# Splitting the products of the second attention into halves, and four small moves around the scan layer and the final norm

## The reference, cut to what matters

```python
def second_block(x, ...):
    # i = 0: scan layer, then keys and values for all later layers
    x = mamba2_layer(x, a_norm_g, a_w_in, conv_w, conv_b, ..., gate_norm_g, w_out)
    k, v = shared_kv_2(x, kv_norm_g, w_kv)
    # i = 1: second attention
    x = diff_attention_layer(x, k, v, norm_g, w_in, lam_qk, sub_g, w_out, lambda_init)
    return rms_norm_2(x, final_norm_g)

def diff_attention_layer(x, k, v, norm_g, w_in, lam_qk, sub_g, w_out, lambda_init):
    qg = rms_norm_2(x, norm_g) @ w_in          # 1024 columns of queries, 1024 of gates
    ...
    scores = einsum("bhiqd,bhikd->bhiqk", qb, k) * scale - slopes * dist     # i = 0, 1
    probs = softmax(where(allowed, scores, -inf))
    weights = probs[:, :, 0] - lam * probs[:, :, 1]
    out = einsum("bhqk,bhke->bqhe", weights, v)
    out = rms_norm_2(out, sub_g) * (1.0 - lambda_init)
    return x + (out * silu(gate)) @ w_out

def mamba2_layer(...):
    zxbcdt = rms_norm_2(x, norm_g) @ w_in      # z, x, B, C and 32 columns of dt
    ...                                        # convolution, chunked scan in 8 groups
    y = gated_group_rms_norm(y, z, gate_norm_g)  # a norm in each of the 8 groups
    return x + y @ w_out
```

## Time and profile before

| | us |
|---|---|
| median of three runs | 2121.86 |
| the profiled execution | 2124.95 |
| its span in the trace | 2123.1 |
| PE busy | 2009.2 (95%) |
| DVE busy | 1387.2 (65%) |
| ACT busy | 856.8 (40%) |
| POOL busy | 267.7 (13%) |
| mean granted clock of PE | 0.972 |

### The profile page before, as it was taken

The page is one execution under the profiler, slowest core; times in us unless marked ns, Lnnn a source line. Parts: engine busy times, 40 slices in busy tenths (PEclk is TensorE's granted clock), DMA queues, the critical chain, the costliest instruction groups (busy, mean ns, idle before and its releaser), DMA issues.

```text
span 2123.1 us, 24820 instructions
## 1 busy us (share of the span) xinstructions
PE 2009.2 (95%) x9332; PEld 1577.4 (74%) x9332; DVE 1387.2 (65%) x2060; ACT 856.8 (40%) x1332; POOL 267.7 (13%) x241
## 2 busy tenths in 40 slices
PE   6789999999999999999999999899999999999987
PEld 4667878888888776777888887677777777876555
DVE  7895457636644448747635654888888887346865
ACT  4454333222233347733222233444444444235653
POOL 4130000000000000010000001234333332000002
PEclk9986999999999999999999999999999999999998
DMA  5354323232233220022233223121222213321002
GB/s 197 107 134 111 122 72 101 85 113 91 86 92 111 88 90 10 1 90 89 85 104 101 96 82 109 53 65 56 80 73 77 80 56 104 101 79 50 21 26 75
DMA packets 79479, 178.33 MB, mean 84 GB/s; under 512 B 17664, under 2 KB 31104, under 8 KB 79360
## 3 DMA queue, kind: packets, MB, share of 16 engines
q1 hardware_dynamic: 75648, 169.46, 26.0%
q0 software_dynamic: 3424, 6.23, 1.1%
q10 hardware_dynamic: 288, 1.05, 0.2%
HBM read 169.43 MB, written 7.27 MB: 83 GB/s over the span
## 4 chain that ended last, share of the span: by engine, by line
PE 74%; DVE 14%; ACT 6%; issue 4%; DMA 1%; POOL 0%; SPq 0%; POOLq 0%; DVEq 0%; ACTq 0%
PE psum L410 19%; PE psum L413 19%; PE psum L411 18%; DVE wl L381 2%; PE psum L430 2%; PE psum L431 2%; PE psum L433 2%; PE psum L780 1%; PE psum L782 1%; PE psum L781 1%; ACT wh L370 1%; PE psum L1617 1%; PE psum L978 1%; DVE S L2451 1%; DVE Bs L2009 1%
## 5 line engine op out<-in xcount | busy, mean ns | idle before, releaser
L381 DVE TENSOR_TENSOR wl<-raw,wh 128x1024 fp32r<-128x1024 f32 (+3 forms) x337 | 387.6, 1151 | 385.6 <-ACT wh L370 385.1
L410 PE MATMUL psum<-xh,wh 128*128 128x512 f32 x1480 | 590.3, 399 | 3.6 <-DVE ust L592 1.8
L413 PE MATMUL psum<-xh,wl 128*128 128x512 f32 x1480 | 579.7, 392 | 1.9 <-DVE wl L381 1.9
L411 PE MATMUL psum<-xl,wh 128*128 128x512 f32 x1480 | 578.7, 391 | 0.0
L370 ACT ACTIVATE wh<-raw 128x1024 fp32r<-128x1024 f32 (+3 forms) x337 | 315.4, 937 | 290.3 <-PE psum L413 181.3
L410 PEld LDWEIGHTS psum<-xh,wh 128*128 128x128 f32 x1480 | 279.7, 189 | 78.3 <-issue 13.6
L413 PEld LDWEIGHTS psum<-xh,wl 128*128 128x128 f32 x1480 | 279.2, 189 | 63.6 <-DVE wl L381 4.5
L411 PEld LDWEIGHTS psum<-xl,wh 128*128 128x128 f32 x1480 | 279.5, 189 | 59.7 <-issue 2.9
L529 POOL TENSOR_TENSOR rs<-rs,sq 128x512 f32<-128x512 f32 x49 | 67.2, 1371 | 1123.7 <-ACT sq L514 1123.0
L410 PE MATMUL psum<-fh,wh 128*128 128x512 f32 x352 | 139.1, 395 | 0.0
L413 PE MATMUL psum<-fh,wl 128*128 128x512 f32 x352 | 139.1, 395 | 0.0
(11 more groups left out here) (449 smaller groups left out, 3099.5 us busy)
## 6 DMA issues: line engine op xcount, KB each, us to landing
raw<-d_w SPq DMA_DIRECT2D x224, 512.0 KB, 3.5
raw<-d_w SPq DMA_DIRECT2D x32, 384.0 KB, 3.0
raw<-d_w SPq DMA_DIRECT2D x48, 256.0 KB, 2.6
raw<-d_w SPq DMA_DIRECT2D x32, 320.0 KB, 2.9
Mt<-d_kd SPq DMA_DIRECT2D x64, 64.0 KB, 2.4
bc<-d_bc SPq DMA_DIRECT2D x8, 256.0 KB, 3.6
d_ud<-ust SPq DMA_DIRECT2D x8, 256.0 KB, 2.6
U<-d_ud POOLq DMA_DIRECT2D x64, 32.0 KB, 2.4
```

The lines of the kernel that those rows point to most:

```text
L381: dve.e.tensor_tensor(K.wl[n % NH][:, 0:COLS[n]], K.raw[n % RAW][:, 0:COLS[n]], K.wh[n % NH][:, 0:COLS[n]].bitcast(F32), ALU.subtract).the ...
L410: pe.e.matmul(b[:, :], WH[:, o:o + P], XH, start=(k == k0), stop=False)
L411: pe.e.matmul(b[:, :], WH[:, o:o + P], XL, start=False, stop=False)
L413: mm = pe.e.matmul(b[:, :], WL[:, o:o + P], XH, start=False, stop=(k == k1 - 1))
```

## The change

In `att2_order` each of the 14 products becomes two steps in neighbouring iterations: the first four slices (12 matmuls) in the old iteration, the other four one iteration later, after that iteration's scores. The new `product_half` issues them into the same bank, and other matmuls go to other banks between them. What reads the result moves one iteration later (`queryB`, `gateB`, `gateT`, `gateC`). The splits get steps of their own: the high part (`H`) at the end of the iteration before the first half, the low part (`L`) behind `combine` in the iteration of the first half. `sumsq` is listed at the head of the iteration after, which is the same place in PE's own order.

In the scan layer, `norm` of group 7 comes before `out` 2 of that group, and the low parts of group 6 are made by DVE and no more by POOL. At the layer's start, ACT loads the table of Ln and Exp ahead of its splits, and DVE takes the variance ahead of its splits.

In the final norm, POOL adds six squares and not seven, and PE sums the seventh with a matmul of its own into the same bank.

```diff
@@ mamba_order
-            ("update", 7, 0), ("update", 7, 1), ("squares", 7, 0), ("scale", 6, 0), ("out", 7, 2), ("sums", 7, 0),
-            ("out", 7, 3), ("norm", 7, 0), ("root", 7, 0), ("newton", 7, 0), ("scale", 7, 0), ("out", 7, 4)]
+            ("update", 7, 0), ("update", 7, 1), ("squares", 7, 0), ("scale", 6, 0), ("norm", 7, 0), ("out", 7, 2),
+            ("sums", 7, 0), ("out", 7, 3), ("root", 7, 0), ("newton", 7, 0), ("scale", 7, 0), ("out", 7, 4)]
@@ att2_order
-    at = {(k * 31 + 6) // 13: x for k, x in enumerate(dense)}
+    first = {(k * 31 + 6) // 13: x for k, x in enumerate(dense)}
+    second = {n + 1: x for n, x in first.items()}
     out = [("query", 0), ("queryB", 0), ("query", 1), ("queryB", 1)]
+    out.append((first[0][0] + "H", first[0][1]))
...
-        if n in at:
-            what, m = at[n]
-            out.append((what, m))
+        if n in first:
+            out.append(first[n])
+        if n in second:
+            what, m = second[n]
+            out.append((what + "2", m))
             later.setdefault((n + 1, "first"), []).append((what + "B", m))
...
             out.append(("combine", n - 2))
+        if n in first:
+            out.append((first[n][0] + "L", first[n][1]))
         if 0 <= n - 3 < 32:
             out.append(("keep", n - 3))
+        if n + 1 in first:
+            out.append((first[n + 1][0] + "H", first[n + 1][1]))
+        if 0 <= n - 3 < 32:
             if (n - 3) % 4 == 3:
                 hd = (n - 3) // 4
-                for k, what in enumerate(("mix", "sumsq", "rs", "tailA", "tailB", "split")):
-                    later.setdefault((n + 1 + k, "last"), []).append((what, hd))
+                for k, what in ((1, "mix"), (3, "rs"), (4, "tailA"), (5, "tailB"), (6, "split")):
+                    later.setdefault((n + k, "last"), []).append((what, hd))
                 later.setdefault((n + 2, "first"), []).append(("square", hd))
+                later.setdefault((n + 3, "first"), []).append(("sumsq", hd))
@@ new
+def product_half(K, pe, name, m, bank, x, freed, half):
+    if half == 0:
+        take(pe, bank, freed)
+        pe.begun = next_unit(K, pe, name, "T", m, 0)
+    n, WH, WL = pe.begun
+    b = K.bank[bank]
+    pe.wait_ge("hi", n + 1)
+    for k in range(4 * half, 4 * half + 4):
+        o = k * P
+        XH, XL = x(k)
+        pe.e.matmul(b[:, :], WH[:, o:o + P], XH, start=(k == 0), stop=False)
+        pe.e.matmul(b[:, :], WH[:, o:o + P], XL, start=False, stop=False)
+        pe.wait_ge("lo", n + 1)
+        mm = pe.e.matmul(b[:, :], WL[:, o:o + P], XH, start=False, stop=(k == 7))
+    if half:
+        mm.then_inc(K.S["unit"], 1)
@@ add_squares, sum_squares
-    for k in range(1, 8):
+    for k in range(1, 7 if b == 6 else 8):
...
-    pe.wait_ge("acc", 7 * (b + 1))
+    pe.wait_ge("acc", 7 * b + 6 if b == 6 else 7 * (b + 1))
...
-    pe.e.matmul(K.bank[bank][:, :], K.con("ones"), K.acc[:, :], start=True, stop=True).then_inc(K.S["ssum"], 1)
+    mm = pe.e.matmul(K.bank[bank][:, :], K.con("ones"), K.acc[:, :], start=True, stop=(b != 6))
+    if b == 6:
+        pe.wait_ge("sq", 8 * b + 8)
+        mm = pe.e.matmul(K.bank[bank][:, :], K.con("ones"), K.sq[1][:, :], start=False, stop=True)
+    mm.then_inc(K.S["ssum"], 1)
@@ mamba_first_act, mamba_first_dve
+    act.log_exp()
     split_hi(K, act, UNIT[("a_w_in_2", "N32", 6144, 0)] + 1 + LA)
...
+    variance(K, dve, 4, 5, 1e-5)
     split_lo(K, dve, UNIT[("a_w_in_2", "N32", 6144, 0)] + 1 + LA)
-    rsqrt(K, dve, 4, 5, 1e-5)
+    dve.wait_ge("ny", 5)
+    newton(K, dve, K.ny[:, :], K.nv[:, :], K.ns[:, :], K.rs[:, :]).then_inc(K.S["rs"], 1)
@@ scan_scale_dve, mamba_pool
-        if g == 7:
+        if g >= 6:
...
-        elif what == "scale" and g < 7:
+        elif what == "scale" and g < 6:
```

More of the change, by code:

```diff
@@ L184, in att2_order @@
     dense = [x for m in range(8) for x in ([("query", m + 2)] if m < 6 else []) + [("gate", m)]]
-    at = {(k * 31 + 6) // 13: x for k, x in enumerate(dense)}
-    assert len(at) == 14 and max(at) < 33
+    first = {(k * 31 + 6) // 13: x for k, x in enumerate(dense)}
+    second = {n + 1: x for n, x in first.items()}
+    assert len(first) == 14 and max(second) < 33 and not set(first) & set(second)
     out = [("query", 0), ("queryB", 0), ("query", 1), ("queryB", 1)]
+    out.append((first[0][0] + "H", first[0][1]))
     later = {}
@@ L571, in newton, with variance @@
     return dve.e.scalar_tensor_tensor(out=out, in0=s, scalar=1.5, in1=y, op0=ALU.add, op1=ALU.mult)
+def variance(K, dve, b, bank, eps):
+    dve.wait_ge("ssum", b + 1)
+    dve.e.tensor_scalar(K.nv[:, :], K.bank[bank][:, :], 1.0 / D, eps, ALU.mult, ALU.add).then_inc(K.S["nv"], 1)
 def rsqrt(K, dve, b, bank, eps, by_token=None):
@@ L578, in rsqrt @@
         dve.e.tensor_scalar(K.tv[:, :], K.bank[by_token][:, 0:4], 1.0 / D, eps, ALU.mult, ALU.add).then_inc(K.S["tv"], 1)
-    dve.wait_ge("ssum", b + 1)
-    dve.e.tensor_scalar(K.nv[:, :], K.bank[bank][:, :], 1.0 / D, eps, ALU.mult, ALU.add).then_inc(K.S["nv"], 1)
+    variance(K, dve, b, bank, eps)
     if b in BY_TOKEN:
@@ L2592, in att2_pe @@
     for what, m in ATT2_ORDER:
-        if what == "query" and m > 1:
-            product(K, pe, "b_w_in_2", m, B2[(what, m)], x, ("aqc", m + 1))
-        elif what == "gate":
-            product(K, pe, "b_w_in_2", 8 + m, B2[(what, m)], x, ("agg", m + 1))
+        if what in ("query", "query2") and m > 1:
+            product_half(K, pe, "b_w_in_2", m, B2[("query", m)], x, ("aqc", m + 1), int(what == "query2"))
+        elif what in ("gate", "gate2"):
+            product_half(K, pe, "b_w_in_2", 8 + m, B2[("gate", m)], x, ("agg", m + 1), int(what == "gate2"))
         elif what == "out":
@@ L2622, in att2_act @@
     for what, m in ATT2_ORDER:
-        if what in ("query", "gate", "out"):
-            split_hi(K, act, done(*tile2(what, m)) + LA)
+        if what in ("queryH", "gateH", "out") or (what == "query" and m < 2):
+            split_hi(K, act, done(*tile2(what.strip("H"), m)) + LA)
         elif what == "gateT":
@@ L2663, in att2_dve @@
     for what, m in ATT2_ORDER:
-        if what in ("query", "gate", "out"):
-            split_lo(K, dve, done(*tile2(what, m)) + LA)
+        if what in ("queryL", "gateL", "out") or (what == "query" and m < 2):
+            split_lo(K, dve, done(*tile2(what.strip("L"), m)) + LA)
         elif what == "queryB":
```

## The result

The changed kernel takes 2091.61 us, the median of four runs (2090.12 to 2093.63), against 2122.31 us for the kernel before in the same session (2120.57 to 2123.85): a ratio of 0.9856, interval 0.9839 to 0.9873. It is faster by 30.7 us. The forecast was 15.5 us and its range ended at 2096, 4.4 us above what came. The profiled execution took 2093.63 us with a span of 2091.8, so the traces differ by 31.3 us of span.

What follows compares the result with a forecast made beforehand. PE, busy 95% of the span, was taken to bound the kernel. Savings of 12.3 (loop), 0.4 (scan start), 1.5 (scan end) and 1.3 us (final norm) summed to 15.5, giving a median of 2106.4 us; range 2096 to 2115.

Steps and rivals of the forecast that it cites:

- Loop, halves: Second attention's loop: 28 half products give PE work in 27 iterations instead of 14, cutting idle time; about 8 us saved.
- Loop, the splits' places: Second attention's loop: moving high and low parts removes VectorE's 32.0 us stand; counted as nothing beyond PE's other gains.
- Loop, idle of what remains: Second attention's loop: five iterations left without a half product keep 1.4 us of PE idle each, 7 us.
- Loop, clock: Second attention's loop: 21.6 us at 1.2 GHz lose 10.8; about half spared, 5 us, bounds 0 and 9.
- Loop, openings and table loads: Second attention's loop: 14 more product openings cost 1.7 us; four more ScalarE table loads, 5.1 us, hidden in spare time.
- Behind the loop: After the second attention's loop: gate 7's second half lies ahead of head 6's sum of squares; 1 us saved.
- Scan layer, start: Scan layer's start: earlier table load and variance let Newton begin sooner; 0.4 us saved taken, possibly 0.6 us lost.
- Scan layer, end: Scan layer's end: group 7's earlier variance shortens the 2.77 us wait before the last pair; 1.5 us saved, bounds 0 and 2.8.
- Final norm: Final norm: GpSimd's last addition goes, so PE starts sooner after ScalarE's last square; 1.3 us saved, bound 0.7.
- More: Rival, chance 0.07: clock stays up in the loop and at both scan layer ends, loop idle down to 4: 2095 us.
- The three on the other side: Rivals of smaller or no gain: VectorE sets pace, 2114 (0.16); loop gives nothing, 2118.7 (0.08); ScalarE sets pace, 2132 (0.04).
- Waits only move: Rival, chance 0.16: VectorE becomes the loop's pace, so the loop gives only 2 to 7 us: 2114 us.

Runs made afterwards that it cites:

- Filler: Kernel before's second-attention loop, ends as changed, plus three unread PE matmuls in each of 18 iterations without a product: 2118.38 us against 2122.35.
- old loop: Changed kernel with the second attention's list as in the kernel before; scan layer and final norm as changed: 2116.38 us against 2122.35.
- late variance: Changed kernel with `norm` of group 7 back behind `out` 3, low parts of group 6 still on VectorE: 2095.42 us against 2123.13.
- whole products: Changed kernel with each product issued whole in its old iteration, splits kept at their new places: 2098.39 us against 2122.35.
- sums behind scores: Changed kernel with each head's `sumsq` behind its iteration's scores and product half instead of ahead of them: 2094.09 us against 2122.84.
- norm undone: Changed kernel with the scan layer's start and the final norm both as in the kernel before: 2095.91 us against 2122.84.

## Why the forecast was wrong, point by point

- **Direction and ranking of the parts: right.** The loop carries most. Against that, the low parts' move to VectorE lost 0.3 us, halves gained nothing without the splits' places, and the places, priced at nothing, gained most.
- **Loop, halves: the failed step, with the next.** "Saved: about 8 us" was priced as cover for PE, with 5 us of clock beside it and 1.7 against it. Halves alone gave nothing (158.2 us against 156.2). At the new places they are worth 7.1, of which 4.1 are idle time and 3.4 clock, but on a condition that the sum did not hold: that the stand is gone.
- **Loop, the splits' places: the step that failed.** "VectorE was not the bound, so I count nothing beyond what PE gets back above." The places alone give 16.4 us. The 32.0 us of the earlier trace rows, 26.2 of them in the loop, were read as harmless because VectorE is busy only 108.9 of 154.1, though the paragraph on the earlier trace rows had named what is queued behind them. Filler cost nothing, so PE was not the pace in the iterations without a product; the round through three engines in order was, and the stand was the link whose removal gave the time.
- **Loop, idle of what remains.** The five iterations without a half were given 1.4 us each, 7 in all. Measured: 3.65 in the whole loop, 2.39 of them at the entry. So 11.1 us of idle time went, where 8 were counted.
- **Loop, clock.** The 21.6 us at the lower level came from the rounded 0.93; the stretches in the trace are 20.5, with 10.2 lost. 5 us were counted as spared, and 8.5 were (10.2 - 1.7). Every stretch at the lower level but the entry's went. But the filler run shows that these losses were no term of their own in the old loop: 3.5 us less lost there returned nothing.
- **Loop, openings and table loads: no cost to be seen.** 1.7 us were subtracted for openings. There are 16 loads, and the waits' list names no wait of PE for them, as forecast; with the splits at their old places they may have cost something (see the halves there).
- **Behind the loop**: 1 us forecast, 2.9 measured, of which 1.2 came with the old loop too: luck in part.
- **Scan layer, start**: 0.4 forecast, 1.3 measured. Small product and low parts went as computed, and the wait ended at 1.01 (1.1 forecast). The 6.8 us at 1.2 GHz that followed it are gone too. They gave back only some 0.6 us (24.84 to 24.25 from the first dense matmul to the first chunk matmul); VectorE is busy 23.8 of these 24.3 us and so is the likely pace there.
- **Scan layer, end**: 1.5 forecast, 3.3 measured. The wait came to 1.06 (1.2 forecast). The term left out the clock: the 6.8 us at 1.2 GHz went with the wait, and that is the larger half of what came (2.0 of 2.8 in the run with the late variance).
- **Final norm**: 1.3 forecast, 1.3 measured.
- **Rivals.** "More" had the right kind and side (clock stays up, idle down to 4) and gave 2095, with a chance of 0.07. The three on the other side did not come true: PE's waits shrank, VectorE was not full (84%), and ScalarE's four loads did no visible harm. "Waits only move" is what halves did at the old places, where PE's wait for `small` rose from 3.7 to 13.1.

## What to carry to other kernels

A stand of an engine that is far from full is not free when it works in order: read what is queued behind the waiting instruction and who waits for that, and price the stand by them, not by the engine's busy share. Where one engine consumes at once what another has just made at the end of its backlog, pull the two apart by one stage, on either side, before adding cover for the engine at the end. A short wait of PE can cost twice where PE sets the pace, since the clock fell behind most waits of 2.3 us and more here, though not behind all; where another engine set the pace, less of either gave back little or nothing.

## What the runs showed of the hardware that was not expected

- The loop's granted clock was 0.99 with 3.65 us of PE idle in 132.7, 0.92 with 14.9 in 156.2, and 0.95 with 6.6 in 156.7 (filler).
- A stretch at 1.2 GHz stood behind the wait of 2.39 us at the entry (3.4 us long) and behind one of 2.48 at the last pair (6.8 us). Waits of 1.06 us at the last pair and 1.01 at the scan layer's start left the clock at 1.00.
- A wait of that size did not always bring it. PE waits 2.34 to 2.37 us before the sums of group 7 in all fourteen traces; in nine a stretch of 3.4 us at 1.2 GHz follows, in five (old loop, whole products, halves at the old places, filler, sums behind scores) the clock stays at 1.00. Before the final norm's sum a wait of 2.85 us left two matmuls at 1.13 us in the kernel before and at 2.07 in the run with the norm undone. No run shows what decides.
- VectorE's instructions beside a GpSimd addition or subtraction took 1.63, 1.75 and 1.37 us where they take 0.69, 0.74 and 0.43 alone, and giving the low parts of group 6 to the one engine or the other changed the stretch by 0.3 us (12.66 and 12.33).
